# Transpose of a growing triangular inverse: recomputed by its own update on VectorE, or taken from the inverse by TensorE and copied by ScalarE

## The reference, cut to what matters

```
sa = S a_t
S  = S diag(w_t) + sa b_t^T + v_t k_t^T
y_t = S r_t
```

## Time and profile before

| what | value |
|---|---|
| median of three runs | 3305.36 us |
| the profiled execution, its own time | 3305.41 us |
| span from its first to its last instruction | 3303.6 us |
| mean granted TensorE clock | 0.935 of full |
| TensorE matmul busy | 2969.5 us, 90% |
| VectorE busy | 1090.3 us, 33% |
| ScalarE busy | 954.6 us, 29% |
| GpSimd busy | 407.5 us, 12% |
| the 32 units | from about 750 us to about 1762 us |

### The profile page before, as it was taken

One profiled execution on the slowest core, in us unless ns is written; L12 is line 12 of the kernel. 1 busy time (PEld: TensorE's weight loads), 2 busy tenths in 40 slices (PEclk: granted clock), 3 DMA queues, 4 the chain that ended last, 5 costly groups with the idle time before them and its releaser, 6 DMA issues. The chain is left out here.

```text
span 3303.6 us, 62866 instructions
## 1 busy us (share of the span) xinstructions
PE 2969.5 (90%) x27318; PEld 2390.3 (72%) x27318; DVE 1090.3 (33%) x2430; ACT 954.6 (29%) x1797; POOL 407.5 (12%) x398
## 2 busy tenths in 40 slices
PE   6888797889999999999987999988999999999797
PEld 3666676856666666666655666687999999999785
DVE  1120202216777777777762111013111111111222
ACT  2120202025555555555542000013122221222212
POOL 0000001002111111112110000011221212212010
PEclk8889796599999999999988999999999999999898
DMA  3211102210001001001001110020111111111011
GB/s 135 80 61 58 70 14 78 105 27 23 25 11 33 19 17 33 19 17 33 13 3 47 42 41 30 12 103 26 45 38 44 44 38 44 38 44 44 29 40 61
DMA packets 57474, 139.18 MB, mean 42 GB/s; under 512 B 5008, under 2 KB 37008, under 8 KB 52400
## 3 DMA queue, kind: packets, MB, share of 16 engines
q1 hardware_dynamic: 53376, 116.03, 10.4%
q10 hardware_dynamic: 3888, 20.05, 1.8%
HBM read 119.54 MB, written 16.54 MB: 41 GB/s over the span
## 5 line engine op out<-in xcount | busy, mean ns | idle before, releaser
L1535 PE MATMUL psum<-hT,rkv_w 128*64 128x256 f32 (+1 forms) x3072 | 412.3, 395 | 11.2 <-DMA rkv_w<-in_w_pair 9.9
L1535 PEld LDWEIGHTS psum<-hT,rkv_w 128*64 128x64 f32 x3072 | 213.0, 138 | 115.6 <-issue 31.3
L129 PE MATMUL psum<-hT,merge_w 128*128 128x352 f32 x768 | 232.3, 463 | 12.2 <-DMA merge_w<-in_w_mix 12.2
L1856 POOL TENSOR_TENSOR ff_w_low<-ff_raw,ff_w_high 128x1024 fp32r<-128x1024 f32 x64 | 157.2, 2457 | 678.1 <-ACT ff_w_high L1851 678.1
L129 PEld LDWEIGHTS psum<-hT,merge_w 128*128 128x128 f32 x768 | 147.3, 192 | 95.1 <-issue 15.2
L152 PE MATMUL psum<-ff_high,ff_w_high 128*128 128x352 f32 x768 | 173.4, 335 | 38.7 <-DVE ff_low L2155 38.7
L2158 DVE TENSOR_TENSOR rwkv_out<-rwkv_out,psum 128x1056 f32<-128x1056 f32 x64 | 80.3, 1254 | 321.3 <-PE psum L152 321.3
L152 PE MATMUL psum<-h_high,ff_w_high 128*128 128x352 f32 x768 | 167.7, 327 | 12.9 <-DVE h_low L226 12.5
L152 PE MATMUL psum<-ff_low,ff_w_high 128*128 128x352 f32 x768 | 170.5, 332 | 0.0
L152 PE MATMUL psum<-ff_high,ff_w_low 128*128 128x352 f32 x768 | 170.0, 330 | 0.0
L1851 ACT ACTIVATE ff_w_high<-ff_raw 128x1024 fp32r<-128x1024 f32 x64 | 67.3, 1052 | 347.7 <-PE psum L152 347.7
(11 more groups left out here) (315 smaller groups left out, 5244.1 us busy)
## 6 DMA issues: line engine op xcount, KB each, us to landing
ff_raw<-in_w_ff SPq DMA_DIRECT2D x64, 512.0 KB, 3.5
merge_w<-in_w_mix SPq DMA_DIRECT2D x8, 1664.0 KB, 6.9
rkv_w<-in_w_pair SPq DMA_DIRECT2D x24, 512.0 KB, 4.1
rwkv_out<-in_kc ACTq DMA_DIRECT2D x4, 2048.0 KB, 12.9
ple_w<-in_w_ple SPq DMA_DIRECT2D x8, 640.0 KB, 3.8
x_in<-in_xT SPq DMA_DIRECT2D x2, 2112.0 KB, 10.8
rwkv_out<-in_xT ACTq DMA_DIRECT2D x1, 4224.0 KB, 13.5
out_yT<-y SPq DMA_DIRECT2D x8, 528.0 KB, 3.1
```

The lines of the kernel that those rows point to most:

```text
L129: last = nc.tensor.matmul(acc[:, n, 0:TT], w[:, k, :], x[:, k, n * TT:(n + 1) * TT], start=k == 0, stop=k == kt - 1)
L1535: mm = nc.tensor.matmul(ahead[half[a], 0:width(v)], w3[:, k, n * P + a * C:n * P + a * C + C], hT[:, k, cols(v)], start=k == 0, stop=k == ...
L1856: return nc.gpsimd.tensor_tensor(parts[1][:, s, :], raw[:, s, 0:KT * P], parts[0][:, s, :].bitcast(F32), ALU.subtract)
```

## The change

X's transpose is no longer updated for itself on levels 0 to 4. At level i (1 to 5), straight behind G_i, TensorE multiplies X by the identity (T_(i-1): 8 matmuls, stationary X, moving identity) into columns 256 to 383 of banks 1 and 2, and ScalarE copies that into XT (`turned(u, i - 1)`). W_i and WT_i wait for this copy. WT and its addition on VectorE stay at level 5 only. `turn` and the four VectorE instructions of level 0 are gone. The value rows are issued at level 1, behind the waits and ahead of W_1, and no longer in `after(2)`. T_1 at level 2 waits for ScalarE's value copies (`v1`). Five copies are put into ScalarE's order.

```diff
-        straight, turned_lt = bank(4)[...], bank(2)[...]
+        straight = bank(4)[:, 0:QT].rearrange("p (c t) -> p c t", c=QC)
+        turn = Blocks(psum[:, 1:3, QT:QT + QT // 2])
@@ ScalarE
+                def turned(u, i):
+                    pe_q.wait(act, f"T{i}", u)
+                    act_q.done(f"xt{i}", nc.scalar.activation(XT[:, :, :].rearrange("p (b c) t -> p b (c t)", b=2), turn[:, slice(0, QC), :], ACT.Copy))
@@ ScalarE, unit
+                    turned(u, 0)
                     keys(u)
                     if valid(p):
                         centres(p)
+                    values(u)
+                    turned(u, 1)
                     if valid(v):
                         rate(v)
                         squares(v)
-                    values(u)
                     if valid(u + 3):
                         evacuate(u + 3, "k")
+                    turned(u, 2)
                     if valid(v):
                         key_scale(v)
+                    turned(u, 3)
+                    if valid(v):
                         key_log(v)
                     if valid(p):
                         var_log(p)
+                    turned(u, 4)
+                    if valid(p):
                         var_root(p)
@@ VectorE, level 0: four instructions out
-                    for h in range(2):
-                        vec_q.done(f"xa{h}", ...)
-                    pe_q.wait(vec, "turn", n)
-                    vec_q.done("xc", ...)
-                    vec_q.wait(vec, "xc", n)
-                    vec_q.done("xt0", ...)
@@ VectorE, levels 1 to 5
-                        pe_q.wait(vec, f"WT{i}", n)
-                        vec_q.done(f"xt{i}", nc.vector.tensor_tensor(XT[:, :, :], inv[2], XT[:, :, :], ALU.add))
+                        else:
+                            pe_q.wait(vec, f"WT{i}", n)
+                            vec_q.done(f"xt{i}", nc.vector.tensor_tensor(XT[:, :, :], inv[2], XT[:, :, :], ALU.add))
@@ TensorE, inverse
                         pe_q.done(f"G{i}", last)
-                        if i == 0:
+                        if i == 1:
                             ... (the waits for the sample steps in bank 2)
-                            for c in crossed: ... turn ...
-                            pe_q.done("turn", last)
+                            vec_q.wait(pe, "rb1", n)
+                        if i == 2:
+                            act_q.wait(pe, "v1", n)
+                        if i:
+                            for c in order:
+                                last = heads(turn, other, X, None, own, c)
+                            pe_q.done(f"T{i - 1}", last)
                         after(i)
                         if i == 0:
                             continue
                         vec_q.wait(pe, f"g{i}", n)
+                        act_q.wait(pe, f"xt{i - 1}", n)
+                        if i == 1:
+                            value_rows(n)
                         if i < LEVELS - 1:
                             for c in order:
                                 last = heads(inv[1], own, XT, Gs, other, c)
                             pe_q.done(f"W{i}", last)
+                            continue
                         for c in order:
                             last = heads(inv[2], other, Gs, XT, other, c)
@@ TensorE, unit
-                        if i == 2:
-                            value_rows(u)
```

More of the change, by code:

```diff
@@ L809, in rwkv_pairs @@
         inv = [*(Blocks(psum[:, 4:6, m * QT // 2:(m + 1) * QT // 2]) for m in range(2)), bank(2)[:, 0:QT].rearrange("p (c t) -> p c t", c=QC)]
-        straight, turned_lt = bank(4)[:, 0:QT].rearrange("p (c t) -> p c t", c=QC), bank(2)[:, QT:2 * QT].rearrange("p (c t) -> p c t", c=QC)
+        straight = bank(4)[:, 0:QT].rearrange("p (c t) -> p c t", c=QC)
+        turn = Blocks(psum[:, 1:3, QT:QT + QT // 2])
         RH, UU, SS = inv[0], inv[1], bank(5)[:, QT:2 * QT].rearrange("p (c t) -> p c t", c=QC)
@@ L840, in rwkv_pairs @@
         vec_z = turns("vec_zero", ["z0", "z1"])
[L842 to L849, removed]
+        rows_at = {1: ["tk", "vt"]}
+        inv_pe = ["G0"] + [m for i in range(1, LEVELS) for m in (f"G{i}", f"T{i - 1}", *rows_at.get(i, []), f"W{i}" if i < LEVELS - 1 else f"WT{i}")]
+        inv_vec = ["g0", "x0", "rb0", "rb1"] + [m for i in range(1, LEVELS) for m in (f"g{i}", f"x{i}" if i < LEVELS - 1 else f"xt{i}")]
         pe_g = turns("pe_gram", ["gram0", "gram1"])
         vec_h = turns("vec_first", ["r0", "r1", "a0", "a1", "pc", "l0", "l1", "m0", "m1"])
-        pe_q = turns("pe_quad", [*inv_pe(LEVELS, ["turn"]), *[f"{m}{c}" for c in range(QC) for m in ("rhs", "u", "s", "y")]])
-        vec_q = turns("vec_quad", [*inv_vec(LEVELS), *[f"{m}{c}" for c in range(QC) for m in ("rhs", "u0", "s0", "s1")]])
-        act_q = turns("act_quad", ["kb", "v0", "v1", *[f"{m}{c}" for c in range(QC) for m in ("sp0", "sp1", "u1_")], "y"])
+        pe_q = turns("pe_quad", [*inv_pe, *[f"{m}{c}" for c in range(QC) for m in ("rhs", "u", "s", "y")]])
+        vec_q = turns("vec_quad", [*inv_vec, *[f"{m}{c}" for c in range(QC) for m in ("rhs", "u0", "s0", "s1")]])
+        act_q = turns("act_quad", ["xt0", "kb", "v0", "v1", "xt1", "xt2", "xt3", "xt4", *[f"{m}{c}" for c in range(QC) for m in ("sp0", "sp1", "u1_")], "y"])
         pool_q = turns("pool_quad", ["b", "k"])
@@ L1233, in doubling @@
                     split = lambda m: m[:, :, :].rearrange("p (b c) t -> p b c t", b=2)
-                    few = lambda m: m[:, None, :].to_broadcast([m.shape[0], QC // 2, C])
                     pe_q.wait(vec, "G0", n)
@@ L1241, in doubling @@
                     mask_rb(n)
-                    for h in range(2):
-                        vec_q.done(f"xa{h}", nc.vector.tensor_tensor(XT[half[h], 0:QC // 2, :], G[h][half[h], 0:QC // 2, 0:C], few(cst("level0_t")[half[h], :]), ALU.mult))
-                    pe_q.wait(vec, "turn", n)
-                    vec_q.done("xc", nc.vector.tensor_tensor(XT[:, QC // 2:QC, :], turned_lt[:, QC // 2:QC, :], few(cst("level0_t")), ALU.mult))
-                    vec_q.wait(vec, "xc", n)
-                    vec_q.done("xt0", nc.vector.tensor_tensor(XT[:, :, :], XT[:, :, :], over(ident2), ALU.add))
                     fill(0)
@@ L1607, in key_rows @@
                 def key_rows(n):
-                    vec_q.wait(pe, "xa1", n)
+                    vec_q.wait(pe, "rb1", n)
                     for c in range(QC):
@@ L1651, in inverse @@
                                 vec_s.wait(pe, "xt1", n // QUADS)
-                            for c in crossed:
-                                for h in range(2):
-                                    last = nc.tensor.matmul(turned_lt[other(h, c), c, :], ident2[own(h, c), :], LT[own(h, c), c, :], start=True, stop=True)
-                            pe_q.done("turn", last)
+                            vec_q.wait(pe, "rb1", n)
+                        if i == 2:
[4 more added lines that the diff above has]
+                            pe_q.done(f"T{i - 1}", last)
                         after(i)
```

## The result

The kernel after takes 3376.75 us (median of 4 runs, 3375.47 to 3377.67), the kernel before 3303.65 beside it: ratio 1.0221 (95% interval 1.0203 to 1.0239), 73 us slower. The forecast was 3366, slower, in a range of 3335 to 3400.

The account below looks back on a forecast made before the run. TensorE's stream from G to W was taken as the bound, VectorE's work as hidden. 1.15 + 0.14 + 0.70 less 0.1 gave 1.9 us per unit, 61 us over 32 units: 3366 us, range 3335 to 3400.

Parts of the forecast that it names:

- From G to W TensorE streams, and VectorE's mask isn't what W waits for: Each level: W's load follows TensorE's own stream, so removing 1.7 us of VectorE additions per unit gains 0.
- WT lies in the shadow, gain 0: Levels 1 to 4: WT's 0.63 us runs during X's update, so dropping it gains 0.
- T: 5 x 0.23: Between G and W at levels 1 to 5: five T products add 1.15 us per unit to TensorE's stream.
- Value rows +0.14: Moving value rows costs level 1 0.60 us and gives level 2 back 0.46: net +0.14 per unit.
- stand at T_1 0.70: Level 2: TensorE stands 0.70 us before T_1, waiting for ScalarE's value copies; bounds 0 and 1.3.
- Waits of W for the copies, and the late SP: 0: W's waits for T copies cost 0 with fill; level 5's later SP fits by 0.04 us, up to 0.5 otherwise.
- Sum 1.9 per unit: Per unit: 1.15 + 0.14 + 0.70 = 1.99 us, less 0.1 for `turn` and an earlier key maximum.
- Times 32, 61 us: Whole kernel: 1.9 us over 32 units adds 61 us to 3305.4, giving 3366.
- rival D: New TensorE gaps lower the clock; a quarter of the inverse at half clock adds 2.5 us per unit, about 3445; chance 0.05.
- A: VectorE sets the levels and T fits load gaps: 1.0 us less per unit, 3273; chance 0.09.
- B: The wait for the value copies at T_1 is small: 1.2 us per unit, 3344; chance 0.12.
- C: T takes 0.63, giving 3430, or ScalarE comes 0.5 late at the chain, giving 3382; chance 0.08.

Follow-up runs that it names:

- Experiment 1: Kernel before, with VectorE's additions of WT to XT left out at levels 1 to 4, WT still computed: 3305.89 us, ratio 0.9994.
- experiment 2: Kernel before, with both the additions and the WT products of levels 1 to 4 left out: 3313.24 us, ratio 1.0014.
- experiment 6: Kernel after, with one fill step of each of levels 1 to 4 moved from ahead of W to behind it: 3321.91 us, ratio 1.0052.
- 7: Kernel before, with one fill step of each of levels 1 to 4 moved from ahead of W to behind WT: 3313.18 us, ratio 1.0016.
- experiment 5: Kernel after, with value rows back at level 2 behind T_1's copy, and T_2 instead of T_1 waiting for the value copies: 3352.42 us, ratio 1.0139.
- experiment 4: Kernel after, with ScalarE's two value copies put ahead of its centre copies: 3357.83 us, ratio 1.0146.
- experiment 3: Kernel after, with each T product issued twice in a row, same result: 3402.55 us, ratio 1.0290.
- 10: Kernel after, with dummy products into an unused bank in the last three units, which have no fill: 3363.23 us, ratio 1.0170.
- experiment 8: Kernel after, with a fill step behind each W of levels 1 to 4 and value copies ahead of centre copies: 3304.31 us, ratio 0.9993.
- 9: Version of experiment 8, with level 2's last fill step put behind G_2, ahead of T_1's wait: 3307.52 us, ratio 1.0005.
- 12: Version of experiment 8, with dummy products in the last three units: 3290.85 us, ratio 0.9942.

## Why the prediction was right, point by point

- *From G to W TensorE streams, and VectorE's mask isn't what W waits for.* Right. Experiment 1 took 41 us of VectorE's time away and won 0.09 us per unit. That 0.09 is level 4, where the mask did come last; the prediction gave levels 1, 3 and 5 and passed over it. The reading that settled the rest ahead of the result was the load row beside the end of the products ahead of it, against a waits view that named VectorE.
- *WT lies in the shadow, gain 0.* Right: experiments 1 and 2 have the same step. The forecast stopped one step short of saying what follows: the freed shadow is worth about 0.4 us per level when a fill step is moved into it (experiment 6, against 7).
- *T: 5 x 0.23.* Right: 0.23 in the trace, 1.17 per unit more when doubled.
- *Value rows +0.14, stand at T_1 0.70: 0.84 together.* The sum is right and its parts are not. The value rows lengthened level 1 by 0.47, not 0.60, so the move cost 0.01 net; W_1 and G_2 came 0.13 earlier for it, and the stand was 0.85. The two errors cancel for a reason: the end of the value copies sets when T_1 loads, and that was forecast to 0.02 us. Undoing both gave 0.72 in experiment 5, which has a stand of 0.15 of its own at T_2.
- *Waits of W for the copies, and the late SP: 0.* Right in the units with fill: every W loads at least 0.4 us behind the end of its copy, and in the unit above SP ends at 1007.06 and the copy of u starts at 1007.09, 0.02 us behind VectorE's copy of the other half.
- *Sum 1.9 per unit.* 1.885 measured. The 0.1 taken off for `turn` and for an earlier key maximum is right partly by luck: 0.06 came back ahead of G_1, where `turn` was, but the key products at level 4 did not come earlier (0.87 us behind G_4 before, 1.11 after). The rest that came back was the 0.09 of the wait for the mask, which the forecast didn't have.
- *Times 32, 61 us.* This is the mis-sized term: 70.1 us of span. 29 steady units would give 54.7 us, and the step as measured 60.3 for 32. The other 10 us are the clock for the most part, which the forecast kept as rival D at 5% and as all or nothing. It came small: 5.6 us in two dips in the middle, and some of the 12.4 in the last part. With dummies in both kernels the last part differs by 8.1 us (1630.4 to 1622.3), so some 4 us there are the clock's. Of the 8.1, 0.95 and 0.86 us lie in units 29 and 30 (2.4 and 4.4 without dummies), 4.9 between unit 31's mask and the first product behind the units, and 1.4 behind that, where the two kernels are the same. So in units 29 and 30 the change costs less than 1.9, not more: in the kernel before, with dummies, W starts 0.05 to 0.06 us behind the mask at levels 1, 3 and 4 of unit 29, and there VectorE's work did set the time, as the prediction had said it might where fill is missing. In unit 31 it costs more: G to W takes 9.90 us over the five levels, 7.21 before, and half of the difference is at level 1. There T_0 loads 0.85 us behind G_1, not 0.23, and the profile names VectorE's mask of RB as what it waited for, which is the wait for `rb1` that the change put ahead of T_0; the forecast had no term for it.
- *Rivals.* A fell to experiment 1, B to the 0.85 us and experiment 4, C to experiment 3 and to the copy of u at 1007.09.
- The reading that the Trainium skill's page "TensorEngine Tiling (Array Packing)", section "PSUM Bottleneck", suggests (spread the evacuation over ScalarE and VectorE) took 94 us off VectorE, put 59 on ScalarE, and could gain no more than 0.1 us per unit here: evacuation wasn't the bound.

Which of the gaps makes the clock dip is shown only in part, from one profile of each version. In the two long units it followed the stand at T_1, but most of the other units had the same stand and kept the full clock; of the versions with that stand in full, after, 3 and 10 had dips in units 1 to 28, and 6 had none; of those in which it was shortened or gone (4, 5, 8, 9, 12) none had one.

## What to carry to other kernels

Look where the work lies before you move it: what an idle engine loses isn't a gain, and what is taken from a busy engine's shadow is free time at the wrong place until something from outside the shadow is moved in. A gap in the weight-load row needn't be a wait of TensorE; compare the load's start with the end of the products ahead of it, on every level, for one of five was a wait after all. A new writer into a shared PSUM bank brought a wait for the bank's last reader here, and the order of that reader's engine set its price.

## What the runs showed of the hardware that was not expected

Less work on TensorE went with a slower kernel (experiment 2: step the same, units 29 and 30 together 7 us longer), and useless work made it faster: 72 dummy steps in the last three units brought 6.5 us in the kernel before, 10.8 in the kernel after and 13.7 in the version of experiment 8, with the granted clock there at 0.96 and 0.91 in place of 0.57 and 0.60. The Trainium skill's page "TensorE: Matmul & The Clock Gate", section "Part 1: The HAM clock gate", says that activity releases the throttle; the traces agree, in both directions.
